# Column sums of squares split between GpSimd and TensorE, and a new order of small attention steps, in a two-model float32 kernel on one core

## What is computed

```python
def rmsnorm(x, g):
    return x * lax.rsqrt(jnp.mean(x * x, axis=-1, keepdims=True) + EPS) * g

for l in range(2):
    proj = rmsnorm(h, norm_mix[l]) @ w_in[l]
    main, mq = proj[..., :768], proj[..., 768:]
    if l == 0: main_out = pool_mixer(main, pool_w, pool_scale)       # windows of 2, 4, 8, 16
    else:      main_out = swa_sink_attention(rmsnorm(q), rmsnorm(k), v, sinks)   # 12 heads, 3 groups
    mkv = rmsnorm(mem, mem_norm[l]) @ w_mem_kv[l]
    mem_out = memory_attention(rmsnorm(mq), rmsnorm(mk), mv)         # softmax over 256 rows
    h = h + concatenate([main_out, mem_out]) @ w_out[l]
    h = h + sq_relu_mlp(rmsnorm(h, norm_mlp[l]), w_up[l], w_down[l])
```

## Time and profile before

| | us |
|---|---|
| median of three runs | 1098.68 |
| lowest, highest | 1096.1, 1110.41 |
| the profiled execution | 1097.39 |
| its span, first to last instruction | 1095.2 |
| TensorE busy in the span | 1033.4 |
| VectorE, ScalarE, GpSimd busy | 688.3, 549.0, 109.2 |

### The profile page before, as it was taken

How to read it: one execution, slowest core, us unless ns; L and a number is a source line. 1 busy time by engine, 2 the same in 40 slices (tenths; PEclk the granted TensorE clock), 3 DMA queues, 4 the chain that set the end, 5 groups by cost and what they waited for, 6 DMA issues and landing times.

```text
span 1095.2 us, 20506 instructions
## 1 busy us (share of the span) xinstructions
PE 1033.4 (94%) x8561; PEld 989.6 (90%) x8561; DVE 688.3 (63%) x807; ACT 549.0 (50%) x714; POOL 109.2 (10%) x64
## 2 busy tenths in 40 slices
PE   4989899899999899999989999999999998999998
PEld 3988689899787899999979899999998888999998
DVE  4667455554476787777777665555576756555553
ACT  4555435443454555555546444444476464544442
POOL 0050021200020000000049400000020003000000
PEclk9999899999999999999999999999999999999999
DMA  6544233224271456455333256555543323565651
GB/s 248 193 155 154 77 116 105 88 78 155 77 244 47 155 200 223 157 211 209 126 113 125 100 203 221 171 212 175 209 155 116 116 78 116 198 223 166 219 172 59
DMA packets 24803, 168.77 MB, mean 154 GB/s; under 512 B 2753, under 2 KB 3137, under 8 KB 5154
## 3 DMA queue, kind: packets, MB, share of 16 engines
q1 hardware_dynamic: 23616, 164.64, 42.9%
q10 hardware_dynamic: 1122, 3.19, 0.9%
HBM read 166.76 MB, written 1.05 MB: 153 GB/s over the span
## 4 chain that ended last, share of the span: by engine, by line
PE 69%; DVE 13%; ACT 8%; POOL 6%; issue 3%; DMA 1%; POOLq 0%; SPq 0%; ACTq 0%; DVEq 0%
PE G L578 11%; PE G L579 10%; PE G L580 10%; PE D L578 7%; PE D L580 7%; PE D L579 7%; DVE wlo L1694 4%; ACT whi L1191 3%; PE M L579 2%; PE M L580 2%; PE M L578 2%; PE D L812 1%; POOL zp L552 1%; POOL wk L530 1%; DVE cv L2062 1%
## 5 line engine op out<-in xcount | busy, mean ns | idle before, releaser
L1694 DVE TENSOR_TENSOR wlo<-raw,whi 128x2048 fp32r<-128x2048 f32 (+1 forms) x156 | 364.9, 2344 | 143.0 <-ACT whi L1191 142.8
L578 PE MATMUL G<-xh,whi 128*128 128x256 f32 (+1 forms) x1360 | 388.4, 286 | 12.3 <-DVE wlo L1694 5.6
L579 PE MATMUL G<-xl,whi 128*128 128x256 f32 (+1 forms) x1360 | 380.0, 279 | 0.0
L580 PE MATMUL G<-xh,wlo 128*128 128x256 f32 (+1 forms) x1360 | 379.8, 279 | 0.0
L1191 ACT ACTIVATE whi<-raw 128x2048 fp32r<-128x2048 f32 (+1 forms) x156 | 295.6, 1898 | 55.4 <-PE D L580 51.2
L578 PEld LDWEIGHTS G<-xh,whi 128*128 128x128 f32 (+1 forms) x1360 | 257.8, 190 | 22.1 <-DVE wlo L1694 8.6
L579 PEld LDWEIGHTS G<-xl,whi 128*128 128x128 f32 (+1 forms) x1360 | 257.2, 189 | 1.6 <-issue 1.4
L580 PEld LDWEIGHTS G<-xh,wlo 128*128 128x128 f32 (+1 forms) x1360 | 256.9, 189 | 0.0
L578 PE MATMUL D<-hh,whi 128*128 128x256 f32 x688 | 190.1, 276 | 3.0 <-DVE wlo L1694 1.9
L579 PE MATMUL D<-hl,whi 128*128 128x256 f32 x688 | 189.9, 276 | 0.0
L580 PE MATMUL D<-hh,wlo 128*128 128x256 f32 x688 | 189.9, 276 | 0.0
(11 more groups left out here) (376 smaller groups left out, 1356.5 us busy)
## 6 DMA issues: line engine op xcount, KB each, us to landing
raw<-wall_dram SPq DMA_DIRECT2D x152, 1024.0 KB, 4.9
raw<-wnarrow_dram SPq DMA_DIRECT2D x4, 768.0 KB, 4.3
x<-x_dram SPq DMA_DIRECT2D x4, 256.0 KB, 5.6
mem<-mem_dram ACTq DMA_DIRECT2D x1, 1024.0 KB, 5.5
out_dram<-x SPq DMA_DIRECT2D x4, 256.0 KB, 2.5
poolw<-pool_w_dram ACTq DMA_DIRECT2D x1, 576.0 KB, 7.5
cst<-cst_dram ACTq DMA_DIRECT2D x1, 416.0 KB, 9.3
lora<-lora_dram ACTq DMA_DIRECT2D x1, 256.0 KB, 6.3
```

The costliest lines, as they stand in the source:

```text
L578: mm(out, w_h, hi, start=start, stop=False, skip_group_check=skip)
L579: mm(out, w_h, lo, start=False, stop=False, skip_group_check=skip)
L580: return mm(out, w_l, hi, start=False, stop=stop, skip_group_check=skip)
L1694: signal(tt(wlo[:, pan.slot, 0:w], raw[:, pan.slot, 0:w], f32(whi[:, pan.slot, 0:w]), SUB), "w_lo")
```

## The change

- `add_squares`: GpSimd makes two adds that do not depend on each other (tiles 0 and 1 with 2 and 3; tiles 4 and 5 with 6 and 7); each is waited for by itself. TensorE sums the four tiles left (`summed`), for the one-column sums too.
- `hn(0)` and `hn(1)` go to bank D0, and norm 3 stands ahead of hn(0); sum_m(0) stands behind the second half of panel in0m 0.
- turn_p(1) uses the four banks D0 to D3.
- sum_s on ScalarE is a step of its own, root_s, placed behind exp_s for groups 1 and 2.
- soft_s(1) stands ahead of score_s(2), and `ahead` of wout1 0 behind it, no longer ahead of its `begin`.
- ScalarE casts the first narrow panel inside parts(3), behind the second pair.

```diff
+    HEAD_SUM = ("D0", "D0", "M1")
...
-    W += [("panel", PAN["mkv0"] + 1), ("hn_square", 0), ("panel", PAN["in0q"]), ("begin", m0), ("hn", 0),
-          ("square_m", 0), ("turn_mv", 0), ("root", 3), ("sum_m", 0), ("panel", m0),
-          ("ahead", m0 + 1), ("begin", m0 + 1), ("score_m", 0), ("panel", m0 + 1), ("exp_m", 0), ("pool", 3),
+    W += [("panel", PAN["mkv0"] + 1), ("hn_square", 0), ("panel", PAN["in0q"]), ("begin", m0), ("root", 3), ("hn", 0),
+          ("turn_mv", 0), ("square_m", 0), ("panel", m0), ("sum_m", 0), ("ahead", m0 + 1), ("begin", m0 + 1), ("score_m", 0), ("panel", m0 + 1), ("exp_m", 0), ("pool", 3),
...
-          ("panel", q1 + 1), ("square_s", 0), ("ahead", k1), ("begin", k1), ("score_m", 1), ("sum_s", 0), ("panel", k1),
+          ("panel", q1 + 1), ("square_s", 0), ("ahead", k1), ("begin", k1), ("score_m", 1), ("sum_s", 0), ("root_s", 0), ("panel", k1),
...
-          ("begin", q2 + 1), ("ahead", q2 + 1), ("sum_s", 1), ("pv_m", 1), ("exp_s", 0), ("panel", q2 + 1), ("soft_s", 0),
-          ("out_m", 1), ("square_s", 2), ("score_s", 1), ("turn_s", 0), ("sum_s", 2), ("pv_s", 0), ("out_s", 0), ("ahead", o1)]
-    W += [("begin", o1), ("exp_s", 1), ("score_s", 2), ("panel", o1), ("soft_s", 1), ("ahead", o1 + 1), ("begin", o1 + 1),
-          ("exp_s", 2), ("turn_s", 1), ("panel", o1 + 1), ("pv_s", 1), ("soft_s", 2), ("out_s", 1), ("turn_s", 2),
+          ("begin", q2 + 1), ("ahead", q2 + 1), ("sum_s", 1), ("pv_m", 1), ("exp_s", 0), ("root_s", 1), ("panel", q2 + 1),
+          ("soft_s", 0), ("out_m", 1), ("square_s", 2), ("score_s", 1), ("turn_s", 0), ("sum_s", 2), ("pv_s", 0), ("out_s", 0)]
+    W += [("begin", o1), ("exp_s", 1), ("root_s", 2), ("soft_s", 1), ("score_s", 2), ("ahead", o1), ("panel", o1),
+          ("ahead", o1 + 1), ("begin", o1 + 1), ("exp_s", 2), ("turn_s", 1), ("panel", o1 + 1), ("pv_s", 1), ("soft_s", 2), ("out_s", 1), ("turn_s", 2),
...
-            for i in range(1, 4):
-                pool.wait_ge(S(sem), before + i + 1)
-                own(tt(buf[:, 0:2, :], buf[:, 0:2, :], buf[:, 2 * i:2 * i + 2, :], ALU.add))
-            tt(buf[:, 0, :], buf[:, 0, :], buf[:, 1, :], ALU.add).then_inc(S(done), 1)
+            for i in (0, 4):
+                pool.wait_ge(S(sem), before + i // 2 + 2)
+                tt(buf[:, i:i + 2, :], buf[:, i:i + 2, :], buf[:, i + 2:i + 4, :], ALU.add).then_inc(S(done), 1)
...
+        def summed(out, buf, sem, before):
+
+            for k in (0, 1, 4, 5):
+                pe.wait_ge(S(sem), before + 1 + k // 4)
+                ins = mm(out, ones, buf[:, k, :], start=k == 0, stop=k == 5)
+            return ins
...
-            if n == 0 or n >= 3:
-                pe.wait_ge(S("sq_sum" if n else "sq_sum0"), max(n - 2, 1))
-                ins = mm(M[1][:, 0, :], ones, (wk2 if n else wk)[:, 0, :])
+            if n == 0:
+                pe.wait_ge(S("sq_sum0"), 1)
+                ins = mm(M[1][:, 0, :], ones, wk[:, 0, :])
+            elif n >= 3:
+                ins = summed(M[1][:, 0, :], wk2, "sq_sum", 2 * (n - 3))
...
-                    ins = mm(DB[3][:, 0, b:b + 1], wk2[:, 0, b * P:(b + 1) * P], ones[:, 0:1])
+                    for k in (0, 1, 4, 5):
+                        ins = mm(DB[3][:, 0, b:b + 1], wk2[:, k, b * P:(b + 1) * P], ones[:, 0:1], start=k == 0, stop=k == 5)
...
-            pe.wait_ge(S("mem_sum"), 1)
-            mm(M[1][:, 0, :], ones, mwk[:, 0, :]).then_inc(S("mem_st"), 1)
+            summed(M[1][:, 0, :], mwk, "mem_sum", 0).then_inc(S("mem_st"), 1)
...
-            free("M1")
-            mm(M[1][:, :, :], bones, hsq[:, :, :]).then_inc(S("hn_ss"), 1)
-            freed["M1"] = ("hn_read", i + 1)
+            bank = HEAD_SUM[i]
+            free(bank)
+            mm(BANK[bank][:, :, :], bones, hsq[:, :, :]).then_inc(S("hn_ss"), 1)
+            freed[bank] = ("hn_read", i + 1)
...
-                bank = f"D{h}" if l == 0 else f"M{h % 2}"
-                out = DB[h] if l == 0 else M[h % 2]
+                bank, out = f"D{h}", DB[h]
...
                 if n == 3:
                     square(n, i)
+                    if i == 1:
+                        split_to(PAN["in0m"] + 1)
...
-        def sum_s(g):
+        def root_s(g):
             row_root(2 + g, 8 + 8 * g, 8)
```

More of the change, by code:

```diff
@@ L1599, in hn @@
                 act.wait_ge(S("hn"), i)
-            own(ln(hy[:], M[1][:, :, :], bias=eps(EPS6), scale=1.0 / 64))
+            own(ln(hy[:], BANK[HEAD_SUM[i]][:, :, :], bias=eps(EPS6), scale=1.0 / 64))
             signal(fn(hy[:], hy[:], ACT.Exp, scale=-0.5), "hn_y")
@@ L1621, in turn_p @@
                 act.wait_ge(S("turned"), 4 * l + h + 1)
-                signal(fn((ptm0, ptm1)[l][:, h, :, :], (DB[h] if l == 0 else M[h % 2])[:, :, :], ACT.Copy), "copied")
+                signal(fn((ptm0, ptm1)[l][:, h, :, :], DB[h][:, :, :], ACT.Copy), "copied")
         def out_m(l):
@@ L1671, in _ @@
                    "mem_norm": mem_norm, "hn": hn, "turn_mv": turn_mv, "turn_v": turn_v,  "turn_p": turn_p,
-                   "out_m": out_m, "pool_mm": pool_mm, "exp_s": exp_s, "out_s": out_s, "sum_m": sum_m, "sum_s": sum_s,
+                   "out_m": out_m, "pool_mm": pool_mm, "exp_s": exp_s, "out_s": out_s, "sum_m": sum_m, "root_s": root_s,
                    "square_m": square_m, "square_s": square_s, "hn_square": hn_square, "part": part, "ahead": ahead, "ahead_hi": ahead, "exp_m": exp_m,
@@ L2118, in hn @@
             dve.wait_ge(S("hn_y"), i + 1)
-            newton(hy[:], M[1][:, :, :], 64, 1e-6, ht[:], ("hn_read", i + 1))
+            newton(hy[:], BANK[HEAD_SUM[i]][:, :, :], 64, 1e-6, ht[:], ("hn_read", i + 1))
             signal(stt(src[:], src[:], gq8[:, i:i + 1], hy[:], MUL, MUL), "hn")
```

## The result

| | before | changed |
|---|---|---|
| median, us | 1102.27 (20 runs) | 1086.12 (20 runs) |
| lowest, highest | 1095.05, 1111.57 | 1084.3, 1102.11 |
| the profiled execution | 1097.39 | 1086.28 |
| its span | 1095.2 | 1084.5 |

The ratio is 0.9873, with a 95% interval of 0.9844 to 0.9902. The profiled executions differ by 11.1 us, their spans by 10.7; 9.3 had been summed. The medians differ by 16.2 us, where about 10 had been forecast (1098.7 to 1088.5); measured again beside the kernel before, they differ by 11.2 and 12.3. The terms explain the 10.7 alone. What the medians show beyond it no term priced, so it is in part luck that the median came out 2.4 us from the forecast 1088.5.

The account below looks back on a forecast made before the run. TensorE, busy 1033.4 of 1095.2 us, was taken as the bound, with gains only in its idle time. Terms summed to -9.3, 1097.4 to 1088.1; forecast 1088.5, range 1082 to 1096.

Parts of the forecast that it names:

- memory sum: At the memory's sum, TensorE makes four 256-column products in place of one: +1.3 us.
- first layer: First memory layer, 547 to 608: TensorE 1.1 us early, diagonal late by 0.9, a wait of about 2: +0.9 us.
- norms 4 and 5: At these sums, waits of 2.6 and slow clock of 1.7 go, added products cost 1.3 and 2.4: -0.6 us.
- turn in four banks: Second memory layer's turn: TensorE's 1.2 us wait for a copy goes: -1.2 us.
- roots behind exponentials: Sliding window, group 0: exponential starts 2.7 us earlier relative to its data; wait shrinks to 0.1, clock holds: -4.3 us.
- second diagonal: Sliding window, group 1: the 1.9 us wait goes, pv_s(1) and turn_s(2) wait 0.9 more: -1.0 us.
- norm 6: At its sum, 4.6 wait and 1.4 slow clock go, 1.3 products and 0.3 wait are paid: -4.4 us.
- lower bound: First memory layer: if the cast is not late, GpSimd's windows bind, starting 1.0 us earlier: -1.0 us.
- Second rival: Lone add held behind VectorE's splits; norm 4 keeps wait and clock loss, norm 6 half its wait: 1096 us, chance 0.09.
- the other rivals: Wait and clock fall in first memory layer, 1090.5 us, 0.17; GpSimd's windows bind, 1098.5 or 1102.6, 0.03; sums double, 1096.8, 0.03.
- 1.9 us left the clock alone: Before the second diagonal's products: clock 1.00 behind the 1.9 us wait, used against a clock fall in the first layer.

Follow-up runs that it names:

- the halves: Kernel before with only the new sums: ratio 1.001, 2.5 us longer by stretches; changed kernel with the three old sum functions back: 0.9947, 3.5 us shorter than before.

## Why the prediction was right, term by term

Each term with what the two profiles show, in us. The measured ones add up to the 10.7 between the spans.

| term | predicted | measured |
|---|---|---|
| memory sum (end of the eight-tile sum) | +1.3 | +1.0 |
| first layer (A and B) | +0.9 | -0.7 |
| norms 4 and 5 (C, and up to the second layer's turn) | -0.6 | -0.3 |
| turn in four banks | -1.2 | -1.5 |
| roots behind exponentials (2.6 wait, 1.7 clock) | -4.3 | -4.3 |
| second diagonal | -1.0 | -0.3 |
| norm 6 (E) | -4.4 | -4.6 |

*Memory.* The +1.0 can't be counted as shown: the eight-tile sum ended between 542.3 and 543.8 in the three profiles of the changed kernel, and at 540.8 and 541.3 in two variants with the same new memory sum.

*First layer: the term with the wrong sign.* The cast came late as worked out: VectorE stood idle for 1.89 us for it and ended the second split at 573.6, as forecast. But behind that the order gave back the delay, and the diagonal stood at 581.91, as late against 580.98 as the whole stage was (1.0). TensorE did not come 1.1 early either: it came at 583.2 and waited 0.3. The early cast of the first narrow panel did not free the wait that it was to free, because VectorE's split of it met GpSimd's second add and took 2.72 us where the next took 1.75, so that wait for the low part stayed at 0.9. What really sets the end of A is GpSimd: from its first window to TensorE's last window product it takes 41.05 us before and 41.07 after, 40.9 to 41.2 in every kernel here. The prediction named this as its lower bound and took the diagonal instead. Against the end of the eight-tile sum the windows began 26.15 us later before, 26.03 after, 24.4 with the old sums in the new order, 27.7 with the first layer as before, 29.3 with the new sums alone. So in A the order and the early cast brought 1.7, the sums of norm 3 took 1.5 of it, and the two cancel. The last two kernels differ ahead of the windows in the early cast alone, so with the new sums and the old order that cast was worth 1.6, though it removed no wait in the changed kernel.

*Norms 4 and 5.* Norm 4 (C) gave -2.75, norm 5 +2.2 up to the head sum behind it and +0.3 behind that: the parts were sized rightly. The -0.6 is a near cancellation that the kernel with the old sum at norm 5 avoids.

*Second rival.* The prediction gave 0.09 to the lone add being held behind VectorE's splits, and counted as evidence against it that two adds had been done in 4.75 us beside two splits. In that row the first of the two adds had begun ahead of the splits; the lone add now takes 3.2, the upper end of what was written (1.4 to 3.3). The changed kernel escaped the rival, but two experiments fell into it at norm 4 (5.73 us). The time was right partly because of which instruction was served first, and that was not in the argument. The margin is thin even so: at norms 4 and 6 the second add ends 0.8 us after TensorE comes, and the two products that fill this take 0.9.

*Roots, turn, norm 6.* Mechanism and size as predicted, with the reversed edits giving 3.6 and 1.3 in D and, in the kernel with the new sums alone, 4.6 in E.

*Second diagonal: right mechanism, mis-sized.* The wait of 1.9 went and one of 1.86 came at pv_s(1), behind ScalarE's exponentials and copies, where 0.9 had been taken. The worked-out cover missed that the sum's bank needs the last of the four copies. Counted against before, the move is worth 0.3. Counted against leaving it out of the changed kernel, it is worth 4.7. Both are true: as soon as the roots and the banks bring TensorE forward by 3.4 us, this diagonal is the next limit. The signs for the other rivals did not appear: the windows took 41 us, no sum cost over 0.46 a product (the sign was anything over 0.43, and the 0.46 is norm 4's with its short wait), and no fall of the clock came in the first layer.

## What to carry to other kernels

Cost a step of a bundle against the bundle, not only against the kernel before: here the halves gave +2.5 and -3.5 us and the whole -11.7, because waits that one half removed stood in front of waits that only the other removed. Move work from a helper engine to the bound engine only at the places where the bound engine was seen waiting; the same edit at two places without a wait cost 4 us. Where single executions scatter, cut the trace at fixed points of the program and compare stretches.

## What the runs showed of the hardware

**Two steps between products at one granted clock.** Within a whole feed-forward block the 256-column products start every 0.113 us or every 0.118 us. One program, two executions; windows of 40 us in the first and the second block of the kernel with norms 4 and 6 by four tiles (number of TensorE instructions in brackets, PEclk third from the end):

```profile
400.00:440.00 40.00, 40.00 (x342) 40.00 (x341) 30.19 (x39) 21.91 (x30) 0.00 (x0) 1.00 0.53 189
660.00:700.00 40.00, 40.00 (x355) 40.00 (x354) 21.66 (x16) 17.61 (x15) 0.00 (x0) 1.00 0.59 207
```

and in its second execution:

```profile
400.00:440.00 40.00, 40.00 (x355) 40.00 (x354) 30.52 (x42) 23.85 (x35) 0.00 (x0) 1.00 0.56 208
660.00:700.00 40.00, 40.00 (x342) 40.00 (x341) 21.97 (x14) 16.54 (x13) 0.00 (x0) 1.00 0.54 183
```

Each block at the longer step costs some 6 us, C being 188.5 in place of 181.9. By my estimate from this, with three such blocks, it makes much of the spread of some 15 us between runs of one kernel. The program alone does not decide it, as these two executions show; its cause is open. Whether a program changes the chances is open too, and the runs hint at it: all nine blocks in the three profiles of the changed kernel had the short step, five of the six in the profiles of the kernels with the roots ahead and with the second diagonal behind had the long one, and these two have medians 11.0 and 10.4 us above the changed kernel beside them, where the stretches explain 3.6 and 4.7. It also means that the profiles of before and of the changed kernel, all blocks at the short step, compare fairly.

**GpSimd's adds and VectorE's splits take turns.** A two-tile add takes 1.3 us alone, 3.2 beside one split and 5.73 beside two; the one-tile add took 0.79 at norm 3 of the new order alone and 2.65 beside a split. A split takes 2.29 us alone. In the changed kernel the first split ran its 2.29, the add (begun 0.2 later) ended 1.1 behind it, and the second split took 3.36, longer by that 1.1. With the new sums alone both splits took 2.29 and the add ended 1.1 behind the second. So one stands still for the whole of the other, and the next split can pass a waiting add. An add that began 0.22 us behind a split lost to this one alone in every profile (9 at norm 4, 11 at norm 6). But an earlier start does not decide it: the two adds that lost to both splits had begun 0.13 ahead of the first, and one that began as far ahead in the kernel before, right behind another add at norm 4, ran at once (1.35 us). What decides is open. The Trainium skill (SBUF — State Buffer, section "SBUF: two separate sides") says this of a two-input instruction of VectorE and one of GpSimd that reads SBUF: an exclusive lock held for the whole instruction. The rows agree that one of the two waits for the whole of the other; that the same waiter can lose twice in a row, and to a split that began behind it, is only in the rows.

**The same wait may or may not take the clock.** Behind the wait of 1.86 us at pv_s(1) the clock stayed at 1.00 in the changed kernel, but fell in one of two executions of the kernel with norms 4 and 6 by four tiles (0.72 in 888 to 894) and in the one with the first layer as before (0.79). The prediction's step "1.9 us left the clock alone" is no rule.
